# A fused two-block transformer kernel: one reciprocal for the pooled branch's bands, modulation tiles placed elsewhere, heads turned at k-tile 7

## The reference, cut to what matters

```python
mod = jax.nn.silu(c) @ w_ada[l] + b_ada[l]                 # 2048 x 12288 weights, one row out
shift1, scale1, gate1, shift2, scale2, gate2 = jnp.split(mod, N_MOD, axis=-1)
h = rms_norm(x, norm1_w[l]) * (1.0 + scale1[:, None]) + shift1[:, None]
proj = h @ w_in[l]
u_pool, q, k, v, g_a, g_b = jnp.split(proj, split_at, axis=-1)
y_a = multiscale_pool(u_pool, w_pool[l], pool_scale[l]) @ w_a_up[l]
q = rms_norm(q.reshape(B, S, SB_HEADS, SB_HEAD_DIM), q_norm_w[l])     # and k alike
y_b = stick_breaking_attention(q, k, v) @ w_b_up[l]
merged = jax.nn.sigmoid(g_a) * y_a + jax.nn.sigmoid(g_b) * y_b
x = x + gate1[:, None] * (merged @ w_o[l])
```

## Time and profile before

| | |
|---|---|
| median of 3 runs | 2304.29 us (2303.45 to 2306.67) |
| profiled execution | 2302.39 us, of which the span in the profile is 2301.1 us |
| PE busy | 2225.4 us |
| DVE, ACT, POOL busy | 1462.9, 1075.9, 178.0 us |
| mean granted clock of PE | 0.977 |

### The profile page before, as it was taken

The page is one execution under the profiler, slowest core; times in us unless marked ns, Lnnn a source line. Parts: engine busy times, 40 slices in busy tenths (PEclk is TensorE's granted clock), DMA queues, the critical chain, the costliest instruction groups (busy, mean ns, idle before and its releaser), DMA issues.

```text
span 2301.1 us, 27346 instructions
## 1 busy us (share of the span) xinstructions
PE 2225.4 (97%) x10723; PEld 1828.8 (79%) x10723; DVE 1462.9 (64%) x1847; ACT 1075.9 (47%) x1573; POOL 178.0 (8%) x318
## 2 busy tenths in 40 slices
PE   5888999999998999999999999999999999999997
PEld 5776888888877888888888888888888877877786
DVE  5768877888884666566445456666655536666664
ACT  3233456544436443543443454555554524565553
POOL 0004211122220100010000000100000000000000
PEclk9889999999999999999999999999999989999999
DMA  9987856688884777777565555544445634333233
GB/s 346 334 300 246 286 176 226 220 297 303 311 294 158 244 232 241 228 235 228 180 197 188 189 192 184 184 145 144 144 150 187 217 114 129 108 110 124 98 128 128
DMA packets 242164, 468.53 MB, mean 204 GB/s; under 512 B 14362, under 2 KB 52468, under 8 KB 241396
## 3 DMA queue, kind: packets, MB, share of 16 engines
q1 hardware_dynamic: 213840, 388.79, 51.5%
q0 software_dynamic: 20480, 67.13, 8.6%
q10 hardware_dynamic: 7716, 10.88, 1.4%
HBM read 464.65 MB, written 2.10 MB: 203 GB/s over the span
## 4 chain that ended last, share of the span: by engine, by line
PE 88%; DVE 5%; DMA 2%; issue 2%; ACT 1%; POOL 1%; SPq 1%; ACTq 0%; DVEq 0%
PE banks L612 26%; PE banks L614 25%; PE banks L613 25%; PE banks L623 2%; DMA ada_w<-in_w_ada 2%; PE banks L899 2%; PE banks L911 1%; DVE ada_acc_vec L1668 1%; DVE ada_acc L1629 1%; PE banks L926 1%; PE banks L925 1%; PE banks L924 1%; PE banks L993 1%; SPq L457 1%; ACT w_high L1122 1%
## 5 line engine op out<-in xcount | busy, mean ns | idle before, releaser
L1609 DVE TENSOR_TENSOR w_low<-raw,w_high 128x1024 fp32r<-128x1024 f32 x674 | 821.6, 1224 | 622.2 <-ACT w_high L1122 621.0
L1122 ACT CAST w_high<-raw 128x1024 fp32r<-128x1024 f32 x674 | 701.6, 1046 | 842.3 <-PE banks L614 842.3
L612 PE MATMUL banks<-w_high,act_a_high 128*128 128x512 f32 (+1 forms) x1696 | 693.6, 409 | 17.0 <-DVE act_a_low L1701 13.5
L613 PE MATMUL banks<-w_low,act_a_high 128*128 128x512 f32 (+1 forms) x1696 | 669.0, 394 | 0.0
L614 PE MATMUL banks<-w_high,act_a_low 128*128 128x512 f32 (+1 forms) x1696 | 668.9, 394 | 0.0
L612 PEld LDWEIGHTS banks<-w_high,act_a_high 128*128 128x128 f32 x1696 | 327.7, 193 | 97.5 <-issue 21.0
L614 PEld LDWEIGHTS banks<-w_high,act_a_low 128*128 128x128 f32 x1696 | 326.9, 193 | 69.9
L613 PEld LDWEIGHTS banks<-w_low,act_a_high 128*128 128x128 f32 x1696 | 327.3, 193 | 63.8 <-issue 2.4
L612 PE MATMUL banks<-w_high,act_b_high 128*128 128x512 f32 x640 | 252.2, 394 | 0.5 <-DVE o_chunk L1884 0.5
L614 PE MATMUL banks<-w_high,act_b_low 128*128 128x512 f32 x640 | 250.4, 391 | 0.0
L613 PE MATMUL banks<-w_low,act_b_high 128*128 128x512 f32 x640 | 250.3, 391 | 0.0
(11 more groups left out here) (326 smaller groups left out, 2096.1 us busy)
## 6 DMA issues: line engine op xcount, KB each, us to landing
raw<-in_w_ff SPq DMA_DIRECT2D x128, 1024.0 KB, 5.2
raw<-in_w_in SPq DMA_DIRECT2D x64, 1024.0 KB, 7.0
ada_w<-in_w_ada POOLq DMA_DIRECT2D x256, 256.0 KB, 4.4
raw<-in_b_w_in SPq DMA_DIRECT2D x44, 1024.0 KB, 5.0
raw<-in_a_w_in SPq DMA_DIRECT2D x36, 1024.0 KB, 5.1
ada_first<-in_w_ada SPq DMA_DIRECT2D x64, 512.0 KB, 9.0
raw<-in_w_o SPq DMA_DIRECT2D x16, 1024.0 KB, 7.1
raw<-in_a_w_out SPq DMA_DIRECT2D x16, 1024.0 KB, 5.1
```

The source lines that it names most:

```text
L612: T.matmul(out, xh, wh, start=(c.first and k == 0), stop=False)
L613: T.matmul(out, xh, wl, start=False, stop=False)
L1122: A.copy(WH[:, h % SPL, :, :], split_ap(h)).then_inc(*done("high", h))
L1609: V.tensor_tensor(WL[:, h % SPL, :, :], split_ap(h), WH[:, h % SPL, :, :].bitcast(F32), ALU.subtract).then_inc(*done("low", h))
```

## The change

- `band_count` no longer takes a minimum and then a reciprocal for each of four windows. The reciprocal of the positions is made once, in place, at the start of `in 4`, and each window takes `max(1 / position, 1 / w)`.
- `TILES_IN` moves modulation tiles: `in 4` 8 to 4, `in 6` 10 to 12, `in 7` 8 to 10, each `ga` 6 to 7, each `ua` 3 to 4, the early parts of `wo` 10 to 8 each, the late parts 4 to 3 each, `wo 2` 14 to 12. The total stays at 256. The places of PE's sums move with the tiles.
- The heads are turned at k-tile 7 of the next chunk and no longer at 4. The pooled means move from k-tiles 6 and 10 of `in 7` to 9 and 13, the mixing from 8 and 12 to 11 and 15.

```diff
-MEANS_AT = {6: (2, 3), 10: (0, 1)}
-MIXED_AT = {8: (2, 3), 12: (0, 1)}
+MEANS_AT = {9: (2, 3), 13: (0, 1)}
+MIXED_AT = {11: (2, 3), 15: (0, 1)}
...
-TILES_IN = {**{("in", n): m for n, m in zip(range(EARLY, 8), (12, 8, 12, 10, 8))},
-            **{("ga", n): 6 for n in range(4)}, **{("ua", n): 3 for n in range(4)},
+TILES_IN = {**{("in", n): m for n, m in zip(range(EARLY, 8), (12, 4, 12, 12, 10))},
+            **{("ga", n): 7 for n in range(4)}, **{("ua", n): 4 for n in range(4)},
             **{("gb", n): 11 for n in range(4)}, **{("ub", n): 5 for n in range(4)},
-            **{("wo", n, "early"): 10 for n in range(2)}, **{("wo", n, "late"): 4 for n in range(2)}, ("wo", 2): 14,
+            **{("wo", n, "early"): 8 for n in range(2)}, **{("wo", n, "late"): 3 for n in range(2)}, ("wo", 2): 12,
...
-                if k == 4 and n - 1 in HEADS:
+                if k == 7 and n - 1 in HEADS:
                     heads_turn(n - 1)
-                if n == 7 and k == 6:
+                if n == 7 and k == 9:
                     T.wait_ge(*of("band_less", (3, 1)))
...
-            V.tensor_scalar(rc[:, :], pos[:, :], float(WINDOWS[n]), None, ALU.min).then_inc(*done("band_min", n))
-            V.wait_ge(*of("band_min", n))
-            V.reciprocal(rc[:, :], rc[:, :]).then_inc(*done("band_count", n))
+            V.tensor_scalar(rc[:, :], pos[:, :], 1.0 / WINDOWS[n], None, ALU.max).then_inc(*done("band_count", n))
...
+                V.reciprocal(pos[:, :], pos[:, :]).then_inc(*done("positions_inverse"))
+                V.wait_ge(*of("positions_inverse"))
```

More of the change, by code:

```diff
@@ L49 @@
                 "heads_sums", "sink_exp"),
-    "bands": ("positions_made", "band_min", "band_count", "band_less", "band_begun", "band_made"),
+    "bands": ("positions_made", "positions_inverse", "band_count", "band_less", "band_begun", "band_made"),
     "masks": ("causal_made", "mask_made", "freq_made", "cmp_masks_made", "pool_fill"),
@@ L728, in tensor_program @@
                 ada_sum(c, k)
-                if k == 4 and n - 1 in HEADS:
+                if k == 7 and n - 1 in HEADS:
                     heads_turn(n - 1)
-                if n == 7 and k == 6:
+                if n == 7 and k == 9:
                     T.wait_ge(*of("band_less", (3, 1)))
                     T.wait_ge(*of("pair_free", ("in", 1)))
-                if n == 7 and k == 8:
+                if n == 7 and k == 11:
                     T.wait_ge(*of("pool_w_landed"))
```

## The result

The changed kernel takes 2289.13 us (median of 4 runs, 2287.91 to 2290.06), the kernel before 2303.87 us in the same comparison: a ratio of 0.9938, 95% interval 0.9920 to 0.9955. Five more runs of it later gave 2287.71 us and 0.9935 (0.9922 to 0.9947). It is faster by 14.7 us, 0.6%. The forecast was 2288.9 with faster at 0.92. The profiled execution took 2288.74 us, its span 2287.5 against 2301.1, PE's mean granted clock 0.981 against 0.977.

The account below looks back on a forecast made before the run. PE was taken to bound the kernel, with 19.4 us recoverable from waits on late DVE and their low clock. In-projections 8.2 plus `wo` 7.2 give 15.4 us off 2302.4, plus 1.9 for the median: 2288.9 us, range 2284.5 to 2296.5.

Parts of the forecast that it names:

- What bounds the kernel: PE's waits for late DVE and the low clock around them: 11.7 us in the in-projections, 7.7 in `wo`, 19.4 at most.
- The reciprocal and the new wait at k-tile 6 of `in 4`: One reciprocal ahead of the first rest in `in 4` makes PE wait at k-tile 6: cost 0.7 us.
- The ring: DVE and POOL's closed cycle for each band from `in 4`: falls from 6.2 to 4.5 us, selects kept at 3.7.
- `in 5`: With the turn at k-tile 7, the rest at k-tile 6 is late: cost 1.8 us, in two waits.
- Rival 1: POOL's selects slow down and lengthen the ring: half way 5.5 us more, 2294.4 us; chance 0.17.
- `in 6` and `in 7`: Twelve and ten tiles leave DVE a microsecond or so late at the heads: cost 1.0 us together, bounds nothing to twice 1.5.
- The low clock: Left out for the new waits in `in 5`, neither being as long as 1.02 us, the shortest that brought it.
- `ga` and `ua`: Eight more tiles there cost nothing: 4.7 us of cover before the suffix sums against at most 0.75 more in front.
- `wo`: Fewer tiles up to `wo 2` and later sums give back 7.2 us of 7.7, bounds 7.7 or 4.9.
- rival 2: `wo` stays bound by loads: the 2.44 us load wait returns before `wo 3`'s sum, 2291.3 us; chance 0.12.
- The sum: In-projections 8.2 us and `wo` 7.2, together 15.4 us off 2302.4; with 1.9 for the median, 2288.9 us.
- Rival 4: The turn isn't what held PE: in-projections give only 2 us, `wo` pays in full, 9.2 gained, 2295.1 us; chance 0.05.

Follow-up runs that it names:

- five runs named above: The changed kernel twice (2289.13, 2287.71 us), with the old tables (2295.36), with sums six k-tiles behind (2286.62), and with those sums plus fewer tiles (2283.72).
- the kernel with 10: Changed kernel with sums six k-tiles behind the last tile and tiles in `in 5` and `in 6` cut from 12 to 10, four moved to `ga`: 2283.72 us.

## Why the prediction was right, and where its terms were off

*What bounds the kernel.* Right: what was won came from the waits of the earlier trace rows and the clock behind them. (The sixth wait, 0.53 us in `wo 2`, was in its window's price without being named.) The parts weren't as cleanly tied to single waits as the prediction had them: the reciprocal alone shortened two of them, and the tables alone, which in the in-projections were to take only the sum's wait in `in 4`, left seven shorter waits there.

*The reciprocal and the new wait at k-tile 6 of `in 4`.* 0.7 forecast, 1.00 measured here (0.73 to 2.03 in the five runs named above). Counted from the squares behind `in 3`, at 191.64 us, the product ends at 5.8 (5.7 forecast), the reciprocal at 7.8, the rest at 9.1 (8.9).

*The ring.* 4.5 forecast, 3.75 to 4.28 measured, so the last subtraction ends 25.7 after the start and not 26.9. The forecast kept the selects at the 3.7 us of one window in the earlier trace rows, since they were to keep the company that they had. They didn't: the prediction itself took four tiles out of the rings, and wrote that this gives room and no time. In the earlier trace rows's window POOL's selects had two rests and a tile beside them, now two instructions in each ring. The selects of the second ring and DVE beside them:

```profile
205.73 1.31 POOL L521 TENSOR_SCALAR_AFFINE_SELECT band<-inverse_count 128x256 f32<-128x256 f32 x1 [0.27 <-DVE inverse_count L1722]
207.11 0.74 POOL L524 TENSOR_SCALAR_AFFINE_SELECT band<-band 128x256 f32<-128x256 f32 x1
207.80 0.39 POOL L521 TENSOR_SCALAR_AFFINE_SELECT band<-inverse_count 128x256 f32<-128x256 f32 x1
208.27 0.40 POOL L524 TENSOR_SCALAR_AFFINE_SELECT band<-band 128x256 f32<-128x256 f32 x1
```

```profile
205.56 1.22 DVE L1609 TENSOR_TENSOR w_low<-raw,w_high 128x1024 fp32r<-128x1024 f32 x1
206.69 0.88 DVE L1629 SCALAR_TENSOR_TENSOR ada_acc<-ada_w,cT,ada_acc 128x512 f32<-128x512 f32 x1
```

The last two selects ran while DVE stood idle for 1.12 us with its rest and tile done (its row at 208.70 above), and took 0.39 and 0.40 us. The first two ran beside a rest and a tile, took 1.31 and 0.74, and each ended about 0.3 us after DVE's instruction. With the old tables there are more tiles between, and the rings are longer, 4.25, 4.47 and 4.25 us. The Trainium skill, SBUF — State Buffer, section "Who interferes with whom", calls the port pair that DVE and POOL share an exclusive lock. By that rule a select would stand until DVE's instruction ends, and the trace agrees: 0.39 us beside an idle DVE and up to 1.37 beside a busy one. Rival 1, the longer ring, went the other way: fewer instructions in the ring leave the selects more time alone.

*`in 5`.* 1.8 forecast, none measured. This is the term most off, and it follows from the last: DVE is free at 219.01, 3.4 us behind PE's start of `in 5` (215.60) and not 5.2, and the rest due at 9.1 ends at 9.0.

*`in 6` and `in 7`.* 1.0 forecast, 1.5 measured (1.20 and 0.30), and the upper bound of 3.0 held; in the changed kernel's second profile these were 1.21 and 0.63. The working under it was off. It has DVE start `in 5` about 7 us behind, where its own numbers give 10.9 - 6.8 = 4.1 for the first rest (6.8 is 5.6 for the heads and 1.2 for the rest). DVE was to reach the heads of both chunks a microsecond or so late; it came 2.5 and 1.6 us late, counted from 1.2 us after the chunk's start, where the sum in `in 7` begins in the earlier trace rows. I had named waits for tiles' loads as what can eat the room, 1.1 us before and 4.8 after; that 12 tiles in a chunk are too many is shown by the kernel with 10, where both waits are gone, but how much of it is the loads isn't.

*The low clock.* I left it out since the new waits were to be short. It didn't fall in any of them. But the bound that I gave, the 1.02 us of the shortest wait with a low clock, was no bound: 1.20 and 1.87 us in this same kernel left the clock at 1.00, and 0.91 us in another brought it down. Nor does 1.8 us in two waits put each under 1.02. Here the forecast was lucky as well as right.

*`ga` and `ua`.* Costed at nothing, 0.7 us measured; the attention paid nothing, as said. But with the tiles a sum moved too: piece 3's fell at k-tile 10 of `ga 1`, behind a tile that DVE reaches only after its attention steps, and PE waits 0.46 us there. It is in every profile with the new tables and the sums at four k-tiles, and gone with six. I had looked at what the tiles stand in front of and not at what waits for them. Piece 2's sum also moved from `in 7` into `ga 0`; it costs the same in both.

*`wo`.* 7.2 forecast of 7.7; 6.7 in the changed kernel's profile. There L638 waits 0.82 us in `wo 3` for a tile that itself waited 0.91 us for its load, and by the prediction's own words such a wait counts against it: rival 2 came in small. It appears in one of the ten profiles with the new tables, so it isn't what the tables do as a rule; 7.8 was measured without it (the tables alone, and the changed kernel's second profile).

*The sum.* 8.2 forecast for the in-projections, `ga` and `ua` together, 8.2 measured; 7.2 for `wo`, 6.7. That the first agrees to a tenth is luck. In the changed kernel's second profile the same two stretches gave 7.0 and 7.8. And the errors in single terms cancelled: 1.8 of cost too much in `in 5`, 0.3, 0.5 and 0.7 too little in `in 4`, in `in 6` and `in 7`, and in `ga` and `ua`; the 0.3 left over lies in no wait. The forecast gain was 15.4 us, taken from the profiled execution, with 1.9 added because the median stood that much above it. The spans are 13.6 us apart and the medians 14.7, and the changed kernel's median stands only 0.4 above its profiled execution. So the hit to 0.2 us in the total is luck too; what held is the size of the gain, to about 1 us.

*The parts and the whole.* Alone, the three won 5.7, 8.8 and 2.2 us, together 16.7 where the change won 14.7; taken back, they cost 3.4, 6.2 and about 1. Every part costs less to lose than it won alone. With intervals of 2 to 4 us either way on each, the sums alone don't show it, but the profiles have a reason: the reciprocal alone and the tables alone each kept the clock at 1.00 in `in 4`, where it fell before, and the change can win that once. Rival 4, that the turn isn't what held PE, was wrong of the change as a whole (its 9.2 us against 14.7). But of the turn's own part it is nearly true: moved alone it turned a 4.52 us wait into one of 2.97, and beside the other two parts its worth isn't shown.

**Open.** Whether the turn at k-tile 7 is worth 1 us or nothing. How much of DVE's lateness with 12 tiles in a chunk is late loads. And what decides whether a wait brings the clock down; see below.

## What to carry to other kernels

An engine's lateness is carried from stage to stage: move the work that makes it, or the step that waits for it, and the wait can show elsewhere, as it did when the reciprocal moved. Count all waits from the first stage to the last before believing that one is gone. What paid here was taking work out of the stages, and breaking two long waits into short ones that left the clock alone (the short waits in `wo 3` show that this isn't sure). When a forecast keeps a duration from the old trace, ask whether the same change alters what runs beside it. When small steps are spread by a table, look at who waits for the last of them, and at the rate at which their loads arrive.

## What the runs showed of the hardware that I had not expected

- The clock depends on more than a wait's length. It stayed at 1.00 around waits of 2.03 (in `in 4`, the change with the old tables), 1.87, 1.83 and 1.76 us, and was low in the windows over all waits of 2.11 and more from `in 4` to `wo 3`, but also over the shorter ones of 1.02 and 0.91 (one reciprocal alone) in `wo 3`. At the same place 1.09 (the change with the old tables) and 0.63 (the turn alone) left it alone. First the one window at full clock over the 2.03 us wait, then `wo 3` with the 0.91 us wait (one reciprocal alone) and with the 1.09 us wait (old tables):

```profile
199.00:208.50 9.50, 7.47 (x38) 1.00 0.63 200
```

```profile
676.00:685.00 9.00, 8.09 (x33) 0.81 0.77 252
```

```profile
676.00:685.00 9.00, 7.91 (x40) 1.00 0.74 244
```

- POOL's first selects of one size took 0.39 to 1.38 us, and the short ones ran beside an idle DVE. An estimate from this: four selects of 0.4, with counts of 0.3 and subtractions of 0.5, would make a ring of 2.4 us, where the changed kernel has 3.75 to 4.28. No run has one.
- How long DVE waits for its tiles' loads changes with how close the tiles stand, but not with that alone. From `in 4` to `in 7`, 12 tiles in each of `in 5` and `in 6` gave 2.7 to 5.5 us in eight profiles, 10 in each gave 1.7 and 0.8 in two. Yet 12 and 10 gave 1.1 us in the kernel before, 2.5 with one reciprocal alone, and 4.2 and 4.3 with the turn alone and with the old tables in the changed kernel.
